# Short expert rests in pairs, one in each half of TensorE's columns, with three weight sets in a ring

## The reference

```python
group_probs = softmax(xf @ w_group + b_group)             # 4 groups
p_group, g_idx = top_k(group_probs, 1)
e_logits = (xf @ w_expert + b_expert) of the chosen group # 8 experts in each
p_exp, e_local = top_k(softmax(e_logits), 2)
gate = p_group * p_exp / sum(p_exp)
order = argsort(flat_e)                                   # 2048 rows, sorted by expert
group_sizes = bincount(flat_e, length=32)
hid = silu(ragged_dot(xs, w1, group_sizes)) * ragged_dot(xs, w3, group_sizes)
ys = ragged_dot(hid, w2, group_sizes) * gate
out = segment_sum(ys, tok)
```

## Time and profile before

| | us |
|---|---|
| median of 3 runs | 3527.41 (3527.38 to 3529.32) |
| the profiled execution | 3522.59, its span 3520.5 |
| PE busy | 3287.3 (93%) |
| DVE, ACT, POOL busy | 957.0, 623.0, 502.5 |
| DMA | 461.63 MB, mean 131 GB/s |

### The profile page before, as it was taken

How to read it: one execution, slowest core, us unless ns; L and a number is a source line. 1 busy time by engine, 2 the same in 40 slices (tenths; PEclk the granted TensorE clock), 3 DMA queues, 4 the chain that set the end, 5 groups by cost and what they waited for, 6 DMA issues and landing times.

```text
span 3520.5 us, 30403 instructions
## 1 busy us (share of the span) xinstructions
PE 3287.3 (93%) x11998; PEld 1911.1 (54%) x11998; DVE 957.0 (27%) x1816; ACT 623.0 (18%) x1405; POOL 502.5 (14%) x543
## 2 busy tenths in 40 slices
PE   4998898888958999999995999999999999999999
PEld 2445444787426777777762445547644444444444
DVE  4224345564131111111113314559511000000101
ACT  3001222222211111111112221127420000000000
POOL 2003242543201000000002100017300000000000
PEclk9999999999978999999997999999999999999999
DMA  5445732001109998888865110020111111222222
GB/s 219 143 108 69 202 36 47 1 25 73 72 27 406 380 340 334 334 333 336 335 234 191 60 48 1 25 59 36 72 48 42 36 36 42 78 96 77 95 74 77
DMA packets 248549, 461.63 MB, mean 131 GB/s; under 512 B 27952, under 2 KB 110288, under 8 KB 244944
## 3 DMA queue, kind: packets, MB, share of 16 engines
q1 hardware_dynamic: 222353, 394.19, 33.6%
q0 software_dynamic: 9360, 34.08, 2.6%
q10 hardware_dynamic: 16688, 31.33, 2.4%
HBM read 481.33 MB, written 61.97 MB: 154 GB/s over the span
## 4 chain that ended last, share of the span: by engine, by line
PE 46%; issue 21%; DVE 2%; POOL 2%; DMA 1%; ACT 0%; POOLq 0%; DVEq 0%; ACTq 0%; SPq 0%
PE bank L2844 12%; PE bank L2875 12%; PE bank L2137 5%; PE bank L2717 3%; PE bank L2308 3%; PE bank L2306 2%; PE bank L2640 2%; PE bank L2650 2%; PE bank L230 1%; POOL e_rows L1734 1%; PE bank L2521 0%; PE bank L2518 0%; PE bank L1486 0%; PE bank L2530 0%; PE bank L2182 0%
## 5 line engine op out<-in xcount | busy, mean ns | idle before, releaser
L1792 PE MATMUL bank<-e_w,e_xsT 128*128 128x256 f32 x2240 | 491.5, 380 | 1.6 <-DVE e_xsT L1832 1.6
L1792 PEld LDWEIGHTS bank<-e_w,e_xsT 128*128 128x128 f32 x2240 | 427.1, 191 | 74.9 <-issue 18.2
L2875 PE MATMUL bank<-w_ff,uT 128*128 128x512 f32 x1024 | 441.9, 594 | 3.6 <-DVE hT L2932 3.6
L2844 PE MATMUL bank<-hT,w_ff 128*128 128x512 f32 x1024 | 439.8, 592 | 0.0
L2875 PEld LDWEIGHTS bank<-w_ff,uT 128*128 128x128 f32 x1024 | 195.0, 191 | 250.3 <-issue 244.1
L2844 PEld LDWEIGHTS bank<-hT,w_ff 128*128 128x128 f32 x1024 | 194.4, 190 | 243.9 <-issue 243.9
L1811 PE MATMUL bank<-e_w,e_hidT 128*128 128x512 f32 x560 | 246.1, 592 | 0.0
L485 PE MATMUL bank<-w_in,hT 128*128 128x512 f32 x512 | 225.3, 601 | 4.3 <-DVE hT L397 2.3
L2137 PE MATMUL bank<-w_gla,nT 128*128 128x512 f32 x384 | 169.1, 601 | 1.3 <-ACT nT L2101 1.3
L1811 PEld LDWEIGHTS bank<-e_w,e_hidT 128*128 128x128 f32 x560 | 103.7, 190 | 117.2 <-issue 117.2
L785 PE MATMUL bank<-hT,w_qkv 128*128 128x512 f32 x384 | 167.0, 593 | 0.0
(11 more groups left out here) (450 smaller groups left out, 3817.4 us busy)
## 6 DMA issues: line engine op xcount, KB each, us to landing
e_w<-in_w SPq DMA_DIRECT2D x144, 2048.0 KB
w_ff<-in_w_ff SPq DMA_DIRECT2D x96, 512.0 KB
wa<-in_w_ada SPq DMA_DIRECT2D x24, 1024.0 KB
y_rows<-e_y ACTq DMA_DIRECT2D x35, 512.0 KB, 6.8
y_rows<-zero SPq DMA_DIRECT2D x1, 16384.0 KB, 104.7
w_in<-in_w_in SPq DMA_DIRECT2D x4, 2048.0 KB, 16.0
w_qkv<-in_w_in SPq DMA_DIRECT2D x12, 512.0 KB, 7.0
x_first<-in_x SPq DMA_DIRECT2D x4, 1024.0 KB, 9.7
```

Source lines behind the costliest of these rows:

```text
L1792: t = pe.matmul(experts_up_bank(k, part, j), b.xsT[n][:, f, :], w[:, f, part * HALF:(part + 1) * HALF], start=f == 0, stop=f == NK - 1)
L2844: t = pe.matmul(k.bank[2 * (j % 2) + h][:, :], w[:, f, :], hT[:, f, h * BANK:(h + 1) * BANK], start=f == 0, stop=f == NK - 1)
L2875: t = pe.matmul(k.bank[2 * n + h][:, :], b.uT[:, f, m * P:(m + 1) * P], b.ring[j % SLOTS][:, h * BANK:(h + 1) * BANK], start=f == 0, stop= ...
```

## The change

Rows of an expert are put into full blocks only while more than 64 are left (a block of 65 to 128 rows is a full one). What is left, up to 64 rows, is a rest. Rests are taken two at a time: one pair shares a 128-row unit, the first in rows 0 to 63, the second in rows 64 to 127. In a pair each product is issued twice, once for each half of the stationary columns (64 token columns each), with the weights of that half's expert as moving operand, and the two results go to the two halves of the PSUM partitions.

Up to 31 full blocks (`FULLS`) and 16 pairs are provided for. The order is fixed: two columns of full blocks, then one pair, and so on; each slot of that order is a "unit". Groups of three units stand in a condition on the larger of the two counts (full blocks, rests), and each unit in one of its own; an unused unit within still turns the rows of the unit after it (`skip`). Weights lie in three sets, used by load number; a pair has two loads. Gathers run six ahead where it was eight. The areas are laid out by hand.

For the given routing: units 0 to 17 are six times full, full, pair (loads 0 to 23); unit 18 is the last full block (load 24), 19 is unused (load 25), 20 a pair (26, 27), and 23, 26, 29 and 32 are pairs (30 and 31, 34 and 35, 38 and 39, 42 and 43) with two unused units before each. After unit 32 the rest is left out.

In addition: the whole of `y_rows` (47 blocks) is cleared; the x tiles, the norm weight and all projection weights of `mix` are loaded on ScalarE's queue at its start, and the x tiles are stored and loaded there too, in four buffers; the routing computes the places for both kinds of blocks.

```diff
-BLOCKS = 2 * T // P + NE
+FULLS = 2 * T // (P // 2 + 1)
+BLOCKS = FULLS + NE // 2
...
-    unsure = BLOCKS - 2 * T // P
-    rows = y_rows[2 * T:, :].rearrange("(p b) (r c) -> p (b r) c", p=P, c=P)
-    sy.dma_start(rows, wide(zero[:, :], 1, unsure * D // P)).then_inc(*s.y_cleared.up().inc)
+    rows = y_rows.rearrange("(p b) (r c) -> p (b r) c", p=P, c=P)
+    sy.dma_start(rows, wide(zero[:, :], 1, BLOCKS * D // P)).then_inc(*s.y_cleared.up().inc)
...
+    v.tensor_tensor(b.blk[:, 0:FULLS, :], wide(total[:, 0, :], 1, FULLS), row[:, 0:FULLS].unsqueeze(2).broadcast_to([P, FULLS, NE]), ALU.is_le).then_inc(*V.up().inc)
+    v.tensor_tensor(b.blk[:, FULLS:, :], wide(total[:, 1, :], 1, NE), row[:, 0:NE].unsqueeze(2).broadcast_to([P, NE, NE]), ALU.is_le).then_inc(*V.up().inc)
...
-ROWS_AHEAD = 8
+ROWS_AHEAD = 6
+SETS = 3
+
+
+def experts_units():
+
+    units, load = [], 0
+    for g in range(NE // 2):
+        for column, pair in ((2 * g, False), (2 * g + 1, False), (FULLS + g, True)):
+            if pair or column < FULLS:
+                units.append((column, tuple(range(load, load + 1 + pair)), pair))
+                load += 1 + pair
+    return units
+
+
+UNITS = experts_units()
+UNIT_OF_LOAD = [u for u, (_, loads, _) in enumerate(UNITS) for _ in loads]
...
+def unit_used(used, unit):
+
+    column, _, pair = unit
+    return used[1] > 2 * (column - FULLS) if pair else used[0] > column
...
+    for u, unit in enumerate(UNITS):
+        column, loads, pair = unit
+        there = unit_used(used, unit)
+        for h, load in enumerate(loads):
+            n, table = load % SETS, 2 * column - FULLS + h if pair else column
+            e = sy.value_load(experts[0:1, table:table + 1], min_val=0, max_val=NE - 1)
+            if load >= SETS:
+                sy.wait_ge(*s.up_made(4 * (UNIT_OF_LOAD[load - SETS] + 1)))
+                sy.wait_ge(*up[n](load // SETS))
+                sy.wait_ge(*gate[n](load // SETS))
+            rows = lambda w: io[w][ds(e, 1)].squeeze(0).rearrange("(k p) f -> p k f", p=P)
+            sy.dma_start(b.w1[n][:, :, :], rows("w1"), cond=there, bounds_check="skip_entire_dma").then_inc(*up[n].up().inc)
+            sy.dma_start(b.w3[n][:, :, :], rows("w3"), cond=there, bounds_check="skip_entire_dma").then_inc(*gate[n].up().inc)
+            if load >= SETS:
+                sy.wait_ge(*s.down_made(UNIT_OF_LOAD[load - SETS] + 1))
+                sy.wait_ge(*down[n](load // SETS))
+            sy.dma_start(b.w2[n][:, :, :], rows("w2"), cond=there, bounds_check="skip_entire_dma").then_inc(*down[n].up().inc)
...
+    end = min(at + 3, BLOCKS)
+    with engine.If(used[2] > UNITS[at][0]):
+        for u in range(at, end):
+            with engine.If(unit_used(used, UNITS[u])):
+                work(u)
+            with engine.Else():
+                skip(u)
+        experts_blocks(engine, used, work, skip, rest, end)
+    with engine.Else():
+        rest(at, BLOCKS - at)
+
+
+def experts_matmul(pe, out, xT, weights, start, stop):
+
+    if len(weights) == 1:
+        return pe.matmul(out, xT, weights[0], start=start, stop=stop)
+    for h, w in enumerate(weights):
+        tokens = slice(h * P // 2, (h + 1) * P // 2)
+        t = pe.matmul(out[tokens, :], xT[:, tokens], w, start=start, stop=stop)
+    return t
...
-                    t = pe.matmul(experts_up_bank(k, part, j), b.xsT[n][:, f, :], w[:, f, part * HALF:(part + 1) * HALF], start=f == 0, stop=f == NK - 1)
+                    t = experts_matmul(pe, experts_up_bank(k, part, j), b.xsT[n][:, f, :], [w[m][:, f, cols] for m in sets], f == 0, f == NK - 1)
...
+    def skip(at):
+        pe.wait_ge(*s.half_0_out(4 * (at + 1)))
+        pe.wait_ge(*s.half_1_out(4 * (at + 1)))
+        pe.wait_ge(*got[(at + 1) % ROWS_AHEAD]((at + 1) // ROWS_AHEAD + 1))
+        experts_turn(k, s, b, at + 1, 0)
+        experts_turn(k, s, b, at + 1, 1)
+        pe.drain()
+        pe.sem_inc(s.up_made.sem, 4)
+        pe.sem_inc(s.hid_turned.sem, 2)
+        pe.sem_inc(s.down_made.sem, 1)
...
-        sy.dma_start(b.x[n][:, :], x_dram[n * P:(n + 1) * P, :]).then_inc(*(s.x_got_0, s.x_got_1)[n].up().inc)
...
+    mix_x_load(k, s, b, x_dram, 0)
+    k.nc.scalar.dma_start(b.norm_w[:, :], spread(k.io["final_norm_w"], D)).then_inc(*s.norm_got.up().inc)
+    mix_load(k, s, b, 0)
+    mix_x_load(k, s, b, x_dram, 1)
     for j in (1, 2):
-        mix_load(k, k.nc.scalar, s, b, j)
-    mix_scalar_rows(k, s, b, 0)
+        mix_load(k, s, b, j)
+    for i in (2, 3):
+        mix_x_load(k, s, b, x_dram, i)
+    mix_scalar_rows(k, s, b, x_dram, x_out, 0)
...
+    if i and i + 3 < NT:
+        a.wait_ge(*s.xn_ready(i))
+        a.wait_ge(*mix_x_stored(s)[(i - 1) % 4]((i - 1) // 4 + 1))
+        mix_x_load(k, s, b, x_dram, i + 3)
```

More of the change, by code:

```diff
@@ L1446, in residual_scalar @@
                 a.activation(hT[:, f, (m - 1) * P:m * P], src, ACT.Identity, scale=affine[:, 2, f:f + 1], bias=affine[:, 3, f:f + 1]).then_inc(*s.half_0_out.up().inc)
-Route = namedtuple("Route", "wr br lg eq gp top ix ixf sel hot both a1 a2 a3 earlier cnt full upto0 upto1 first blk ef rank div w2 row_of blk_of hp0 hp1 hb0 hb1 pos lT")
+Route = namedtuple("Route", "wr br lg eq gp top ix ixf sel hot both a1 a2 a3 earlier cnt low left upto0 upto1 first lines whole blk ef place w2 row_of blk_of parts hp0 hp1 hb0 hb1 pos lT")
 NL = GROUPS + NE
@@ L1630, in route_places_vector @@
     ranks = k.bank[1][:, 0:NT * NE].rearrange("p (m e) -> p m e", m=NT)
-    w2, rank, div, a1 = b.w2, b.rank[:, :], b.div[:, :], b.a1[:, :]
+    in_full, in_half, place = b.lines[:, 0, :], b.lines[:, 1, :], b.place[:, :, :]
+    v.tensor_scalar(in_half, b.first[:, 1, :], float(P // 2), float(FULLS * P), ALU.mult, ALU.add).then_inc(*V.up().inc)
+    v.tensor_tensor(place, ranks, wide(b.whole[:, :], 1, NT), ALU.is_lt).then_inc(*V.up().inc)
+    v.wait_ge(*V.now())
+    v.tensor_tensor(in_half, in_half, b.whole[:, :], ALU.subtract).then_inc(*V.up().inc)
@@ L1635, in route_places_vector @@
         v.wait_ge(*V.now())
[L1636 to L1639, removed]
-        v.tensor_reduce(a1, w2[:, :, :], AX.X, ALU.add).then_inc(*V.up().inc)
-        v.wait_ge(*V.now())
-        v.tensor_tensor(w2[:, :, 0:NT - 1], wide(rank, 2, NT - 1), wide(k.c("steps")[:, 1:NT], 1, NT), ALU.is_ge).then_inc(*V.up().inc)
@@ L1682, in used_blocks @@
-def used_blocks(engine, experts):
-    return engine.value_load(experts[0:1, BLOCKS:BLOCKS + 1], min_val=0, max_val=BLOCKS)
+    v.wait_ge(*V.now())
+    v.tensor_scalar(b.parts[:, 0], where[:, :, :], P - 1, None, ALU.bitwise_and).then_inc(*V.up().inc)
+    v.tensor_scalar(b.parts[:, 1], where[:, :, :], 7, None, ALU.logical_shift_right).then_inc(*V.up().inc)
+    v.wait_ge(*V.now())
+    v.tensor_copy(b.row_of[:, :, :], b.parts[:, 0]).then_inc(*V.up().inc)
+    v.tensor_copy(b.blk_of[:, :, :], b.parts[:, 1]).then_inc(*V.up().inc)
@@ L1708, in experts_sync @@
             next(ahead, None)
-    for n in range(2):
+    for n in range(SETS):
         sy.wait_ge(*up[n].now())
@@ L1778, in work @@
     def work(at):
-        n = at % 2
-        pe.wait_ge(*up[n](at // 2 + 1))
+        n, loads = at % 2, UNITS[at][1]
+        sets = [load % SETS for load in loads]
+        for load in loads:
+            pe.wait_ge(*up[load % SETS](load // SETS + 1))
         pe.wait_ge(*s.half_0_out(4 * (at + 1)))
@@ L1783, in work @@
         for part in range(2):
-            for j, w in enumerate((b.w1[n], b.w3[n])):
+            cols = slice(part * HALF, (part + 1) * HALF)
+            for j, w in enumerate((b.w1, b.w3)):
                 if part == 0 and j:
-                    pe.wait_ge(*gate[n](at // 2 + 1))
+                    for load in loads:
+                        pe.wait_ge(*gate[load % SETS](load // SETS + 1))
                 if at:
@@ L1802, in work @@
                 experts_turn(k, s, b, at + 1, 1)
-        pe.wait_ge(*down[n](at // 2 + 1))
+        for load in loads:
+            pe.wait_ge(*down[load % SETS](load // SETS + 1))
         for part in range(2):
@@ L2189, in decay @@
     pe.wait_ge(*mix_s.v_out(NT))
-    v.wait_ge(*mix_s.x_stored_0.now())
-    v.wait_ge(*mix_s.x_stored_1.now())
+    for stored in mix_x_stored(mix_s):
+        a.wait_ge(*stored(NT // 4))
     for m in range(NT):
```

220 lines of the change are left out of this document (112 added, 108 removed).

## The result

The kernel after takes 3483.65 us (median of 4 runs, 3469.89 to 3488.02), beside 3527.39 us for the kernel before (4 runs, 3522.07 to 3529.32): ratio 0.9872, 95% interval 0.9841 to 0.9902. The change gives 44 us, 1.3% and clear of the noise, where 91 were forecast; 3483.65 lies outside the forecast's own range of 3410 to 3465 and inside the wide one of 3405 to 3565. The profiled execution of after took 3480.97 us (span 3478.7), 41.6 us less than that of before.

| part | forecast | measured |
|---|---|---|
| first weight issue of the experts (clearing, route) | +15.1 | +16.6 (1054.90 to 1071.49) |
| stage of the experts, first issue to last eviction | -112 (676) | -70.6 (788.2 to 717.5) |
| last eviction to first projection (gathers, barrier, issues) | +5.7 | +12.1 (41.9 to 54.0) |

What follows compares the result with a forecast made beforehand. TensorE bounds the expert stage before, transfers and load order after. Terms -112 + 12.6 + 2.5 + 3.7 + 2 = -91 us give 3431.4 profiled, 3436 median; own range 3410 to 3465 (chance 0.58), 8-in-10 range 3405 to 3565.

Steps and rivals of the forecast that it cites:

- What bounds the kernel, and the count after: Expert stage: TensorE sets the pace before; after, 24 units for 35 but still 35 weight loads, and TensorE stops being the bound.
- Pair at one block: Expert stage: the column halves of a pair overlap, so a pair costs 22.6 us, a block plus mode changes.
- Rivals A and B: Expert pairs: A, halves take turns, 43.6 us a pair, 3653 us, chance 0.18; B, 1.5 blocks a pair, 3538, chance 0.08.
- Rival C: Expert pairs overlap imperfectly, 1.26 blocks each; TensorE bounds the mixed part again; total 3483 us, chance 0.09.
- Rival D: Expert transfers: three outstanding sets and more gathers in flight drop the rate to 380 GB/s; total 3481 us, chance 0.05.
- The mixed part: Expert loads 0 to 23: full-full-pair periods of 68.7 us at 412 GB/s, first pair ending at 82.6, unit 17 at 426.
- The last four pairs: End of the expert stage: each pair behind two empty units waits for its loads, 48.9 us each, 196 in all.
- Clearing and route: Ahead of the experts: longer clearing of y_rows +12.6 us (bounds 8 and 16), routing and register reads +2.5.
- After the last pair: Behind the experts: eight leftover gathers +3.7 us, loads and issues on ScalarE's queue +2 (bounds 0 and 10).
- a reserve: Expert stage: 2 us added for issues that no row prices, making 676 against 788.2.
- the four cold starts: Last four pairs: the first eight steps run at the half clock, 7.0 us in place of 3.5; without it, stage 666.

Runs made afterwards that it cites:

- the halves in turn: Kernel after, with all products of one column half of a pair issued before those of the other: 3573.96 us, stage 812.6.
- the clearing in two: Kernel after, with 32 of 47 blocks cleared as before and the other 15 behind the convolution's loads: 3470.04 us, first weight issue 1060.74.
- The repeat of after: The kernel after run once more, unchanged, for its own spread: 3482.41 us (3479.75 to 3485.18), ratio 0.9877, stage 717.4.
- the nine kernels: The nine profiled kernels that clear as after does: w_ab product starts at 418.2 to 428.9 us, first weight issue at 1063.2 to 1076.9.
- the two last edits: One full block ahead of the groups, and decay tables from the 23rd unit, added to the four edits together with 8-row leftover fetches: 3359.83 us, ratio 0.9529.
- a better order: Kernel after, with full block g and pair g in turn instead of two full blocks and a pair: 3423.24 us, ratio 0.9709, stage 642.9.

## Why the prediction was wrong

**What bounds the kernel, and the count after: right.** In the mixed part TensorE gave way to the DMA engines, 413 GB/s at share 1.04 against the 412 assumed.

**Pair at one block: right.** 22.5 us where nothing waits (23 to 27 in the mixed part, with its short waits for w3; 22.6 put), and with the halves in turn 32.6. Rivals A and B fall. Rival C's 3483 us is the measured total, but not its mechanism: TensorE isn't the bound in the mixed part, and no pair costs 1.26 blocks of its own work. The Trainium skill, "TensorE: Matmul & The Clock Gate", Part 3, gives three column-packed products 2.38 times the speed, which I had scaled to 1.59 for two; here a warm pair's 32 down records take 7.09 us beside 7.03 for the 16 of a full block, 1.98 times. Rival D falls with the 413 GB/s.

**The mixed part: a term mis-sized, +21.8 us.** The period of 68.7 us was right for 67.9, 67.6, 68.9 and 71.6, beside one of 75.4. But I let it run from TensorE's start and put the first pair's end at 82.6 us; it came at 93.5. The transfers bind from the very first issue: by the time the first pair has both w3, 23.1 MB of weights, 3.1 of the six gathers ahead and some 1.5 of two more and a store have passed, 27.7 MB or 67.2 us, and 2.5 more since the first 16 us carried only 348 GB/s. From 16 us after the first issue to the pair's end the DMA share was 1.03 to 1.05. Its products began at 68.1 and stood 1.0 us more at 73.5, as I read it for w3. They went on at 74.5, when 29.7 MB had moved: transfers behind this w3 were under way too. The gathers ahead were not in the sum, nor were the decay tables (7 us). They are only 0.4 MB, but between 1203.88 and 1220.47 SyncE issued nothing but them, and the DMA engines fell to 83 to 233 GB/s for some 6 us before the next weights came. With 3 us from the last blocks the last pair before the tail ends at 499.8, not 478.

**The last four pairs: mechanism right, size off, +21.7 us.** 54.4 us each, not 48.9. The wait is 29.5 to 30.9 us, not 22.8: I had left out 1.04 us of SyncE between the skipped load and the next. Then 2.8 us pass from the issue to the first weight packet in all four waits, while only the store moves; I had put 2.4 for issue and landing together, from no row. From there it is 25.7 us to TensorE's first product, in place of 20.4: the two gathers take 2.5, the start of the fifth weight transfer (0.65 MB) 1.6, and the last 1.2 I can't part. The pair itself was 24.3 us, not 26.1: its cold products took 15.89 us, 2 above the warm, not 3.5. What I failed to see was not the length but the choice. The empty units between the pairs cost 84 us, and I priced them without asking what they would give back.

**Clearing and route: right in size, in part by luck.** +16.6 for +15.1, and the clearing in two shows that the longer clearing is the cause. But the way was another than I had written. I let the barrier wait for the clearing to land, 22.6 us later than before. It landed 17.5 us later after its issue (122.2 for 104.7), at 415.8, and the barrier opened at 421.4, when SyncE had got through the issues held up behind it. The repeat of after shows the same (418.7, last issue done at 424.04, product at 424.3). I had that only as an upper bound of 16. The two together gave the product +10.7, where I had put 12.6. What is left to the first weight issue is +5.9, where I had +2.5 for the route; over the nine kernels it is +1 to +6.

**After the last pair: mis-sized,** +12.1 for +5.7: 4.8 us for the eight gathers (3.7 put), and 6.9 of 7.3 behind the barrier for ScalarE's held issues, with bounds of 0 and 10, where I had taken 2; moving them gave back 5.6. The load held for 17.4 us in the earlier trace rows, by which I had judged this, was the fifth issue of its row and not the second.

In sum 1.5 + 21.8 + 21.7 - 2 (a reserve) + 6.4 = 49.4 us, against 49.6 between -91.2 and -41.6. The failed step is thus the sum of the stage: the first pair's end and the periods, which left out bytes that pass ahead of and beside the weights, and the length of the last pairs' wait. No term had the wrong sign; I summed TensorE's work closely and the transfers loosely, in a stage that I had just found to be bound by transfers.

A smaller slip: without the four cold starts of 3.5 us the forecast's steps give 662, not 666.

**What stays open.** Why the first four runs of after spread over 18 us and the next over 5; why the first weight packet comes 2.8 us after its issue ahead of the last pairs; and what each of the two last edits gives.

## What to carry to other kernels

When a change moves the bound to the transfers, count from the first issue on every byte that goes through, small ones too: reads ahead, stores, tables, and gathers for work that doesn't exist. An unused slot in a static list isn't free if it keeps its waits: look where it stands between used ones, since a wait that protects nothing there stops the queue behind it. And follow a gain in a stage past its end: a better order moved 17 us of leftover gathers behind the last eviction.

## What the runs showed of the hardware

**Column halves.** Two f32 products on different column halves, issued in turn, run at once: 7.09 us for 32 records where one after another they would take 14.0 (32 of 439 ns). With runs of 8 or 16 records to a half, the totals come out as if some four records overlapped at each change of half, whether of 216 or of 439 ns.

**Small rows in a gather.** A row of 32 bytes takes some 105 ns of a DMA engine (the estimate above), and 15 fetches of 128 such rows, 61 KB in all, cost a stage bound by transfers 17 to 21 us (721.4 against 703.9, and 658.9 against 638.3, where nothing else differs). The Trainium skill, "DMA: Bandwidth & Descriptors", section Specifications, puts the least transfer for full rate at 512 bytes. The trace agrees as far as it goes: 32 bytes in 105 ns are 0.3 GB/s of one engine, beside 26 when all 16 carry 413, and no run tries a size in between.

**An issue behind much outstanding work holds its engine.** SyncE stood 19.64 us in one issue behind the clearing, and 0.40 with a shorter clearing; ScalarE 12.05 and 5.85 us at the start of the mix. That a full queue is the reason is my reading; the traces show only the long issues.
